# Long and short weight products in turns of one instead of two, in the second layer's gate and value stage

## The chip, the cores and the metric

The kernel runs on one NeuronCore of a Trainium2 chip. The metric is the device time of one execution in microseconds; lower is better.

## The reference

A trunk of two layers works on 256 tokens of width 2048, in float32. Each layer has a token mixer (a causal convolution module in the first, differential attention in the second) and then a gated feed-forward part of width 5504:

```python
def conv_ffn(x, w_gate, w_up, dw, dw_b, w_down):
    g = causal_dwconv(x @ w_gate, dw, dw_b)        # width 3, over tokens
    return (jax.nn.silu(g) * (x @ w_up)) @ w_down
```

The change touches the two products `x @ w_gate` and `x @ w_up` of the second layer.

## The kernel before

**Precision.** Every float32 operand of a product is split in two: a rounded part (type fp32r, made by ScalarE) and the remainder (made by VectorE). A product is then the sum of high x high, high x low and low x high. `w_hi` and `w_lo` hold the two parts of the weights, in four buffers of 1024 columns (`PIECES`); `normed` holds the two parts of the activations side by side, 256 columns of high part and 256 of low part for each of 16 tiles of 128 channels.

**The stages.** The work goes through nine stages: conv_in, conv_out, up0, down0, qk, v, wo, up1, down1. A block is 16 weight tiles of 128 x 128 (1 MB); SyncE's DMA queue brings blocks in order into four buffers (`stage`). For each half block ScalarE writes the high part (`hi`, line 553, after a wait that the buffer's last user is done: `pieces_done`), then VectorE the remainder (`lo`, line 903), then TensorE uses both.

**Two kinds of product on TensorE.** In conv_in, conv_out, down0, v, wo and down1 the activations are the stationary operand and 512 columns of weights are moved through the array: three products of 512 columns for each tile (lines 1532 to 1534, in v 1798 to 1800). In up0, qk and up1 the weights are stationary, in `block_mm`: for each of 16 tiles a long product moves all 512 columns (high and low part of the activations) through `w_hi` (`high_product`, line 1498), and a short one moves the 256 columns of the high part through `w_lo` (`low_product`, line 1503), into the second half of the same PSUM bank. Every product loads its own stationary tile first (records PEld). At the block's end ScalarE copies the second half out (line 565), VectorE adds it to the first (lines 1225 and 1254) and does the gate's convolution and the gating (lines 1235 to 1263), and ScalarE its activation (line 772).

**The order of the products.** `block_mm` waits for the PSUM bank (`evacuated`), and for each half block of 8 tiles for VectorE's remainder (`lo_ready`, line 1481). Then it runs tiles in groups of two: long, long, short, short. The last short product of a half block increments `pieces_done`, which gives the weight buffer back to ScalarE.

**The loops.** The stage up1 has 86 blocks, gate and value in turns: four in a first turn written out (the function `up`), 20 turns of four in a loop on the engines (`pe.Fori(1, KF // 2)`, KF = 43), and two at the end. up0 is the same code with the first layer's weights, qk has 32 blocks.

Of the kernel before, what the change touches and what calls it, by code (L numbers as in the profile page):

```python
# [122 lines left out]
def trunk(nc, x_in, positions, norm_mix, norm_ffn, norm_final, conv_w_in, conv_b_in, conv_dw, conv_dw_b,  # L123
# [7 lines left out]
    KD, KF, TB = D // P, F // P, T // P  # L131
# [15 lines left out]
    B, C = {}, {}  # L147
# [41 lines left out]
    with ExitStack() as ctx:  # L189
        def sb(name, shape, dt=F32, stack=ctx):  # L190
            return stack.enter_context(nc.sbuf_tensor("sb_" + name, shape, dt))
# [14 lines left out]
        normed = sb("normed", [P, KD, 2 * T], F32R)  # L206
# [1264 lines left out]

        @block.tensor
        def _(pe):
            def block_mm(i, blocks_per_turn, block_n, chunk_n, operand, arrivals=(), halfway=None):


                bank = chunk_n % BANKS
                pe.wait_ge(evacuated, 4 * i + chunk_n + 1)
                k = 0
                for h in range(2):  # L1480
                    pe.wait_ge(lo_ready, 2 * blocks_per_turn * i + 2 * block_n + h + 1)
                    slot = (2 * block_n + h) % PIECES
                    if h == 1 and halfway:
                        halfway()
                    for q in range(0, KD // 2, 2):
                        for p in (q, q + 1):
                            for tile, count in arrivals:
                                if tile == k + p:
                                    pe.wait_ge(operand_ready, count)
                            high_product(bank, slot, p, operand, k + p, k + p == 0)  # L1490
                        for p in (q, q + 1):
                            ins = low_product(bank, slot, p, operand, k + p, k + p == KD - 1)
                    k += KD // 2
                    ins.then_inc(pieces_done, 1)

            def high_product(bank, slot, q, operand, k, begin):

                nc.tensor.matmul(acc[:, bank, :], w_hi[:, slot, q * P:(q + 1) * P], operand[:, k, :],  # L1498
                                 start=begin, stop=False, skip_group_check=True)

            def low_product(bank, slot, q, operand, k, end):

                return nc.tensor.matmul(acc[:, bank, T:2 * T], w_lo[:, slot, q * P:(q + 1) * P],  # L1503
                                        operand[:, k, 0:T], start=False, stop=end, skip_group_check=True)
# [57 lines left out]
            def turn_resid(name, c):  # L1562

                n = STAT[name]
                pe.wait_ge(evacuated, BANKS + C[name] + TB * (c + 1))
                if c > 0:

                    pe.wait_ge(operand_ready, OPER[name] + 4 * c)
                for f in range(4):
                    k = 4 * c + f  # L1570
                    for b in range(TB):
                        ins = nc.tensor.transpose(aux[:, f, b * P:(b + 1) * P], resid[:, b, k * P:(k + 1) * P],  # L1572
                                                  ident[:, :])
                    ins.then_inc(resid_turned, 1)
# [10 lines left out]
            def stat(n):  # L1585

                pe.wait_ge(diag_row_ready, TB * n)
                for b in range(TB):
                    ins = nc.tensor.matmul(aux[:, 3, T + b * P:T + (b + 1) * P], ones[:, :], diag_row[:, b, :],
                                           start=True, stop=True)  # L1590
                ins.then_inc(stat_ready, 1)
# [24 lines left out]
            def turn_taps(n):  # L1616

                if n == 0:
                    pe.wait_ge(taps_ready, 2)
                    pe.wait_ge(operand_ready, OPER["x"] + KD)  # L1620
                if n >= BANKS:
                    pe.wait_ge(taps_kept, n + 1 - BANKS)
                nc.tensor.matmul(aux[0:HALF, n % BANKS, :], kern_op[:, n % 2, 0:HALF],
                                 taps_op[:, WIDE * (n // 2):WIDE * (n // 2 + 1)], start=True, stop=True
                                 ).then_inc(taps_turned, 1)
# [19 lines left out]
            def forward(c, rows=range(TB)):  # L1645

                if c == 0:
                    pe.wait_ge(dft_ready, 1)
                    pe.wait_ge(par_kept, 3)
                elif c < CH - 1:  # L1650
                    pe.wait_ge(conv_kept, TB * c)
                for b in rows:
                    pe.wait_ge(glu_split, TB * c + b + 1)
                    for m in range(2):
                        triple(aux[0:HALF, 2 * b + m, :], (dft_hi[:, m, 0:HALF], dft_lo[:, m, 0:HALF]),
                               (glu_op[:, b, 0, :], glu_op[:, b, 1, :]), True, True).then_inc(forward_done, 1)

            def inverse(c, banks):

                for b in range(TB):  # L1660
                    for source in range(b + 1):
                        for m in range(2):
                            at = 2 + 2 * (b - source) + m
                            pe.wait_ge(prod_split, 4 * c + 2 * source + m + 1)
                            ins = triple(banks[:, b, :], (dft_hi[0:ROWS, at, :], dft_lo[0:ROWS, at, :]),
                                         (prod_op[0:ROWS, source, m, 0, :], prod_op[0:ROWS, source, m, 1, :]),
                                         source == 0 and m == 0, source == b and m == 1)
                        if b and source == 0:
                            ins.then_inc(source_done, 1)
                    ins.then_inc(inverse_done, 1)  # L1670
# [13 lines left out]
            for at in range(len(ORDER["conv_in"])):  # L1684
                c, j = divmod(at, 8)
                halfway = None
                if at in TAP_TURNS:
                    halfway = lambda: [turn_taps(n) for n in TAP_TURNS[at]]
                elif at == 9:
                    halfway = turn_params  # L1690
                elif c > 0 and j == 2:
                    halfway = lambda: forward(c - 1)
                elif 0 < c < CH - 1 and j == 5:
                    halfway = lambda: inverse(c - 1, aux)
# [35 lines left out]
            def up(name, before):  # L1730

                arrivals = [(0, OPER[name] - 4)] + [(KD - 4 + f, OPER[name] - 3 + f) for f in range(4)]
                block_mm(0, 4, B[name], C[name], normed, arrivals, lambda: turn_resid(before, CH - 1))
                block_mm(0, 4, B[name] + 1, C[name] + 1, normed, halfway=lambda: stat(STAT[before]))
                for j in range(2, 4):
                    block_mm(0, 4, B[name] + j, C[name] + j, normed)
                with pe.Fori(1, KF // 2) as i:
                    for j in range(4):
                        block_mm(i, 4, B[name] + j, C[name] + j, normed)
                for j in range(2):  # L1740
                    block_mm(KF // 2, 4, B[name] + j, C[name] + j, normed)

            def down(name, hidden_name, turn=True):
                base = OPER[hidden_name]
                project(name, hidden, KF, [(0, base + KF - 3), (KF - 3, base + KF - 2), (KF - 2, base + KF - 1),
                                           (KF - 1, base + KF)], turn=turn)

            up("up0", "conv_out")
            down("down0", "up0")

# [92 lines left out]
            def last_heads(at, k):  # L1843
# [5 lines left out]
                elif (at, k) == (1, 1):  # L1849
# [3 lines left out]
                                           (KD - 4, OPER["wo"] - 2),  # L1853
                                           (KD - 2, OPER["wo"])], last_heads)
            up("up1", "wo")
            down("down1", "up1", False)

# [29 lines left out]
```

## Time and profile before

| | |
|---|---|
| median of 3 runs | 2146.43 us (2146.39 to 2147.22) |
| the profiled execution, its own time | 2146.78 us |
| its span | 2145.0 us |
| granted TensorE clock, mean over the span | 1.000 |
| instructions | 30522 |

The profile is one execution. Its span goes from the first to the last instruction; its own time has 1.78 us more around it. PE is TensorE's matmuls, PEld its weight loads, which overlap with matmuls; DVE is VectorE, ACT is ScalarE. Matmuls overlap in the records too: a product's record is longer than the distance to the next one's start, so their spacing is read from starts, not from lengths.

### The profile page before, as it was taken

The numbers are of one execution on the slowest core, as the hardware profiler recorded it, in microseconds if no ns is written. First come the engines' busy times: TensorE is split into PE (matmuls) and PEld (weight loads), VectorE is DVE, ScalarE is ACT, GpSimd is POOL, SyncE is SP. The second block draws the span as 40 slices with busy tenths as digits, with TensorE's granted clock in tenths as the row PEclk, the third lists the DMA queues.
The fourth block names the chain that finished last, engine by engine and source line by source line (L and its number), as shares of the span: only waits on it lengthen the run. The fifth ranks groups of instructions, "written<-read, shape, count | busy, mean of one in ns | idle before, by whom it ended". The sixth has DMA issues, their size and how long they took to land.

```text
span 2145.0 us, 30522 instructions
## 1 busy us (share of the span) xinstructions
PE 2128.6 (99%) x11045; PEld 1815.1 (85%) x11045; DVE 1449.8 (68%) x2130; ACT 1052.2 (49%) x1492; POOL 48.9 (2%) x50
## 2 busy tenths in 40 slices
PE   8999999999999999999999999999999999999998
PEld 7888888888888888888888888888888888888886
DVE  6666767777777774454688867667777777765443
ACT  6554655445444443444554444554444544444443
POOL 7100000000000000000000000000000000000000
PEclk9999999999999999999999999999999999999999
DMA  8555366666666665555656554566666666656553
GB/s 302 176 185 196 128 186 177 195 182 191 188 185 194 185 188 191 192 190 191 189 165 176 180 176 155 193 180 186 186 194 183 190 189 184 194 195 212 191 191 113
DMA packets 513804, 399.07 MB, mean 186 GB/s; under 512 B 6542, under 2 KB 425832, under 8 KB 513392
## 3 DMA queue, kind: packets, MB, share of 16 engines
q1 hardware_dynamic: 513408, 397.91, 60.1%
q8 instruction: 42, 0.69, 0.1%
q10 hardware_dynamic: 336, 0.33, 0.0%
q14 instruction: 18, 0.15, 0.0%
HBM read 396.11 MB, written 2.10 MB: 186 GB/s over the span
## 4 chain that ended last, share of the span: by engine, by line
PE 97%; DVE 2%; ACT 1%; DMA 0%; issue 0%; SPq 0%; DVEq 0%; ACTq 0%
PE acc L1498 35%; PE acc L1503 18%; PE acc L1532 12%; PE acc L1534 12%; PE acc L1533 12%; PE acc L1800 1%; PE acc L1798 1%; PE acc L1799 1%; DVE sb_w_lo L903 1%; PE aux L1572 0%; DMA sb_stage<-in_conv_w_in 0%; PE aux L1641 0%; PE aux L1642 0%; PE aux L1643 0%; PE aux L1809 0%; PE aux L1757 0%
## 5 line engine op out<-in xcount | busy, mean ns | idle before, releaser
L903 DVE TENSOR_TENSOR sb_w_lo<-sb_stage,sb_w_hi 128x1024 fp32r<-128x1024 f32 (+1 forms) x743 | 906.4, 1222 | 519.1 <-ACT sb_w_hi L553 514.6
L553 ACT ACTIVATE sb_w_hi<-sb_stage 128x1024 fp32r<-128x1024 f32 (+1 forms) x743 | 780.5, 1053 | 661.4 <-PE acc L1534 380.5
L1498 PE MATMUL acc<-sb_normed,sb_w_hi 128*128 128x512 f32 x3264 | 1027.4, 396 | 0.0
L1503 PEld LDWEIGHTS acc<-sb_normed,sb_w_lo 128*128 128x128 f32 x3264 | 613.1, 188 | 144.9
L1503 PE MATMUL acc<-sb_normed,sb_w_lo 128*128 128x256 f32 x3264 | 641.4, 278 | 0.0
L1498 PEld LDWEIGHTS acc<-sb_normed,sb_w_hi 128*128 128x128 f32 x3264 | 497.7, 189 | 0.6
L1532 PE MATMUL acc<-sb_w_hi,sb_hidden 128*128 128x512 f32 x674 | 262.5, 389 | 0.0
L1534 PE MATMUL acc<-sb_w_hi,sb_hidden 128*128 128x512 f32 x674 | 262.2, 389 | 0.0
L1533 PE MATMUL acc<-sb_w_lo,sb_hidden 128*128 128x512 f32 x674 | 262.2, 389 | 0.0
L565 ACT ACTIVATE sb_corr<-acc 128x256 f32<-128x256 f32 x204 | 76.9, 377 | 210.7 <-PE acc L1503 210.6
L1534 PEld LDWEIGHTS acc<-sb_w_hi,sb_hidden 128*128 128x128 f32 x674 | 126.5, 188 | 26.4
L1533 PEld LDWEIGHTS acc<-sb_w_lo,sb_hidden 128*128 128x128 f32 x674 | 126.5, 188 | 26.3
L1532 PEld LDWEIGHTS acc<-sb_w_hi,sb_hidden 128*128 128x128 f32 x674 | 126.5, 188 | 25.9
L772 ACT ACTIVATE sb_acted<-sb_scaled,sb_par_f 128x256 f32<-128x256 f32 x86 | 44.0, 512 | 135.2 <-DVE sb_scaled L1245 135.2
L1245 DVE SCALAR_TENSOR_TENSOR sb_scaled<-sb_gate_in,sb_par_f,sb_scaled 128x256 f32<-128x256 f32 x172 | 83.4, 485 | 24.0 <-DVE sb_scaled L1242 3.2
L1532 PE MATMUL acc<-sb_w_hi,sb_normed 128*128 128x512 f32 x248 | 97.1, 391 | 2.4 <-DVE sb_normed L917 2.4
L1533 PE MATMUL acc<-sb_w_lo,sb_normed 128*128 128x512 f32 x248 | 96.6, 390 | 0.0
L1534 PE MATMUL acc<-sb_w_hi,sb_normed 128*128 128x512 f32 x248 | 96.6, 389 | 0.0
L1225 DVE TENSOR_TENSOR sb_summed<-acc,sb_corr 128x256 f32<-128x256 f32 x86 | 36.5, 425 | 73.8 <-ACT sb_corr L565 73.8
L1532 PEld LDWEIGHTS acc<-sb_w_hi,sb_normed 128*128 128x128 f32 x248 | 46.6, 188 | 12.5 <-DVE sb_w_lo L903 2.8
L1534 PEld LDWEIGHTS acc<-sb_w_hi,sb_normed 128*128 128x128 f32 x248 | 46.6, 188 | 9.8
L1533 PEld LDWEIGHTS acc<-sb_w_lo,sb_normed 128*128 128x128 f32 x248 | 46.6, 188 | 9.6
(215 smaller groups left out, 1647.5 us busy)
## 6 DMA issues: line engine op xcount, KB each, us to landing
sb_stage<-in_ffn_w_gate SPq DMA_DIRECT2D x86, 1024.0 KB, 5.4
sb_stage<-in_ffn_w_up SPq DMA_DIRECT2D x86, 1024.0 KB, 5.5
sb_stage<-in_ffn_w_down SPq DMA_DIRECT2D x80, 1024.0 KB, 5.0
sb_stage<-in_attn_w_qkv SPq DMA_DIRECT2D x48, 1024.0 KB, 5.4
sb_stage<-in_conv_w_in SPq DMA_DIRECT2D x31, 1024.0 KB, 5.6
sb_stage<-in_conv_w_out SPq DMA_DIRECT2D x16, 1024.0 KB, 5.1
sb_stage<-in_attn_w_o SPq DMA_DIRECT2D x16, 1024.0 KB, 5.0
sb_stage<-in_ffn_w_down SPq DMA_DIRECT2D x8, 768.0 KB, 4.4
```

Of the source, the lines that this page charges most:

```text
L553: nc.scalar.activation(w_hi[:, (2 * first + h) % PIECES, 0:size], stage[:, first % STAGES, off:off + size], ACT.Copy).then_inc(hi_ready, 1)
L565: nc.scalar.activation(corr[:, chunk_n % BANKS, :], acc[:, chunk_n % BANKS, T:2 * T], ACT.Copy).then_inc(corr_ready, 1)
L772: nc.scalar.activation(acted[:, e, :], scaled[:, e, :], ACT.Silu, bias=par_f[:, layer, bass.ds(FTAPS * KF + f, 1)]).then_inc(gate_acted, 1)
L903: nc.vector.tensor_tensor(w_lo[:, slot, 0:size], stage[:, first % STAGES, off:off + size], w_hi[:, slot, 0:size].bitcast(F32), ALU.subtrac ...
L1225: nc.vector.tensor_tensor(summed[:, 0, :], acc[:, (C[name] + 2 * e) % BANKS, 0:T], corr[:, (C[name] + 2 * e) % BANKS, :], ALU.add).then_in ...
L1245: ins = nc.vector.scalar_tensor_tensor(out=scaled[:, e, :], in0=x, scalar=w, in1=scaled[:, e, :], op0=ALU.mult, op1=ALU.add)
L1498: nc.tensor.matmul(acc[:, bank, :], w_hi[:, slot, q * P:(q + 1) * P], operand[:, k, :], start=begin, stop=False, skip_group_check=True)
L1503: return nc.tensor.matmul(acc[:, bank, T:2 * T], w_lo[:, slot, q * P:(q + 1) * P], operand[:, k, 0:T], start=False, stop=end, skip_group_c ...
L1532: nc.tensor.matmul(acc[:, bank, :], high, w_hi[:, slot, wide], start=k == 0, stop=False)
L1533: nc.tensor.matmul(acc[:, bank, :], high, w_lo[:, slot, wide], start=False, stop=False)
L1534: ins = nc.tensor.matmul(acc[:, bank, :], low, w_hi[:, slot, wide], start=False, stop=k == tiles - 1)
L1798: nc.tensor.matmul(acc[:, bank, :], high, w_hi[:, slot, wide], start=k == 0, stop=False)
```

## The change

A new argument of `block_mm`, `single`, sets the group to one tile, so that long and short products alternate: long, short, long, short. It is passed in the loop of `up` for the second layer's stage (`name == "up1"`) alone; the first turn and the last two blocks of that stage, and the stages up0 and qk, keep groups of two. No instruction is added or left out, and waits and increments stay where they are.

```diff
-            def block_mm(i, blocks_per_turn, block_n, chunk_n, operand, arrivals=(), halfway=None):
+            def block_mm(i, blocks_per_turn, block_n, chunk_n, operand, arrivals=(), halfway=None, single=False):
...
-                    for q in range(0, KD // 2, 2):
-                        for p in (q, q + 1):
+                    group = 1 if single else 2
+                    for q in range(0, KD // 2, group):
+                        for p in range(q, q + group):
                             for tile, count in arrivals:
                                 if tile == k + p:
                                     pe.wait_ge(operand_ready, count)
                             high_product(bank, slot, p, operand, k + p, k + p == 0)
-                        for p in (q, q + 1):
+                        for p in range(q, q + group):
                             ins = low_product(bank, slot, p, operand, k + p, k + p == KD - 1)
...
                 with pe.Fori(1, KF // 2) as i:
                     for j in range(4):
-                        block_mm(i, 4, B[name] + j, C[name] + j, normed)
+                        block_mm(i, 4, B[name] + j, C[name] + j, normed, single=name == "up1")
```

## Rows read from the trace of the kernel before

**Rows 1.** The page's busy time by engine: us (share of span) xinstructions

```profile
PE 2128.6 (99%) x11045; PEld 1815.1 (85%) x11045; DVE 1449.8 (68%) x2130; ACT 1052.2 (49%) x1492; POOL 48.9 (2%) x50
```

**Rows 2.** The page's chain that ended last, shares of the span by line

```profile
PE acc L1498 35%; PE acc L1503 18%; PE acc L1532 12%; PE acc L1534 12%; PE acc L1533 12%; PE acc L1800 1%; PE acc L1798 1%; PE acc L1799 1%; DVE sb_w_lo L903 1%; PE aux L1572 0%; DMA sb_stage<-in_conv_w_in 0%; PE aux L1641 0%; PE aux L1642 0%; PE aux L1643 0%; PE aux L1809 0%; PE aux L1757 0%
```

**Rows 3.** Busy time by stretch, the loop of up1 (columns in the first line)

```profile
core 0: us, PE busy (x) PEld busy (x) DVE busy (x) ACT busy (x) POOL busy (x), PEclk, DMA share, GB/s
...
1444.80:1890.70 445.90, 445.90 (x2563) 389.05 (x2562) 332.87 (x521) 219.85 (x321) 0.00 (x0) 1.00 0.65 189
```

**Rows 4.** Groups of instructions, same stretch: busy us, mean ns | idle before us

```profile
L1498 PE MATMUL acc<-sb_normed,sb_w_hi 128*128 128x512 f32 x1281 | 402.4, 395 | 0.0
L1503 PE MATMUL acc<-sb_normed,sb_w_lo 128*128 128x256 f32 x1282 | 251.8, 278 | 0.0
L1503 PEld LDWEIGHTS acc<-sb_normed,sb_w_lo 128*128 128x128 f32 x1280 | 240.4, 188 | 56.8
L903 DVE TENSOR_TENSOR sb_w_lo<-sb_stage,sb_w_hi 128x1024 fp32r<-128x1024 f32 x161 | 197.0, 1224 | 58.1 <-ACT sb_w_hi L553 57.9
L1498 PEld LDWEIGHTS acc<-sb_normed,sb_w_hi 128*128 128x128 f32 x1282 | 195.1, 189 | 0.0
L553 ACT ACTIVATE sb_w_hi<-sb_stage 128x1024 fp32r<-128x1024 f32 x160 | 169.2, 1057 | 91.8 <-PE acc L1503 91.8
```

**Rows 5.** Waits in the same stretch: us in total, times, longest

```profile
ACT sb_w_hi L553 <- PE acc L1503: 91.8, 80, 1.4
...
DVE sb_w_lo L903 <- ACT sb_w_hi L553: 57.9, 119, 0.8
```

**Rows 6.** Timeline of TensorE (start us, us, what), the loop's first and next products

```profile
1444.82 0.63 PE L1498 MATMUL acc<-sb_normed,sb_w_hi 128*128 128x512 f32 x2
...
1890.68 0.63 PE L1498 MATMUL acc<-sb_normed,sb_w_hi 128*128 128x512 f32 x2
```

**Rows 7.** Timeline, nine products of the loop in order, one by one

```profile
1499.85 0.40 PE L1498 MATMUL acc<-sb_normed,sb_w_hi 128*128 128x512 f32 x1
1500.09 0.39 PE L1498 MATMUL acc<-sb_normed,sb_w_hi 128*128 128x512 f32 x1
1500.32 0.28 PE L1503 MATMUL acc<-sb_normed,sb_w_lo 128*128 128x256 f32 x1
1500.43 0.28 PE L1503 MATMUL acc<-sb_normed,sb_w_lo 128*128 128x256 f32 x1
1500.55 0.40 PE L1498 MATMUL acc<-sb_normed,sb_w_hi 128*128 128x512 f32 x1
1500.78 0.40 PE L1498 MATMUL acc<-sb_normed,sb_w_hi 128*128 128x512 f32 x1
1501.02 0.28 PE L1503 MATMUL acc<-sb_normed,sb_w_lo 128*128 128x256 f32 x1
1501.13 0.27 PE L1503 MATMUL acc<-sb_normed,sb_w_lo 128*128 128x256 f32 x1
1501.24 0.40 PE L1498 MATMUL acc<-sb_normed,sb_w_hi 128*128 128x512 f32 x1
```

**Rows 8.** Timeline, the down projection of the second layer, 180 products apart

```profile
2000.00 0.39 PE L1533 MATMUL acc<-sb_w_lo,sb_hidden 128*128 128x512 f32 x1
...
2040.80 0.39 PE L1533 MATMUL acc<-sb_w_lo,sb_hidden 128*128 128x512 f32 x1
```

**Rows 9.** Timeline, the down projection's first product and its seventh

```profile
1901.83 0.40 PE L1532 MATMUL acc<-sb_w_hi,sb_hidden 128*128 128x512 f32 x1
...
1903.21 0.39 PE L1532 MATMUL acc<-sb_w_hi,sb_hidden 128*128 128x512 f32 x1
```

**Rows 10.** Timeline, first groups of qk, behind the first layer's down projection

```profile
1036.84 0.62 PE L1498 MATMUL acc<-sb_normed,sb_w_hi 128*128 128x512 f32 x2
...
1037.52 0.63 PE L1498 MATMUL acc<-sb_normed,sb_w_hi 128*128 128x512 f32 x2
...
1038.22 0.62 PE L1498 MATMUL acc<-sb_normed,sb_w_hi 128*128 128x512 f32 x2
```

**Rows 11.** Timeline, two weight loads beside the products of rows 7

```profile
1500.32 0.19 PEld L1503 LDWEIGHTS acc<-sb_normed,sb_w_lo 128*128 128x128 f32 x1
1500.43 0.19 PEld L1498 LDWEIGHTS acc<-sb_normed,sb_w_hi 128*128 128x128 f32 x1
```

## The prediction

> **What bounds the kernel now.** I begin with the page's busy line: TensorE's matmuls are busy for 2128.6 of 2145.0 us [rows 1], and the chain that ended last runs through TensorE for nearly its whole length, 35% of the span at the long products of the routine that the change edits and 18% at its short ones [rows 2]. A busy share of 99% alone would not prove a bound, since matmul ends are modelled, so the second thing to look at is whether TensorE ever waits in the stage of the change. The stretch from 1444.80 to 1890.70 us holds the loop of the second layer's gate and value stage: matmuls cover all 445.90 us of it, at a granted clock of 1.00 (the 2.4 GHz level), while VectorE works 332.87 us and ScalarE 219.85 us [rows 3]. The groups of that stretch say the same: no idle time is recorded ahead of either product, each product has a weight load of its own whose record is 188 or 189 ns long, and the makers of the weights (ScalarE's rounded copy, VectorE's remainder) do 169.2 and 197.0 us of work [rows 4]. The list of waits has ScalarE waiting 91.8 us for TensorE to give back weight buffers, and VectorE 57.9 us for ScalarE; nothing is on it that TensorE waits for [rows 5]. So the stage lasts exactly as long as TensorE needs to run its queue of loads and products, and the only thing in this edit that can move the time is the spacing of those products.
>
> **How they are spaced.** The first long product of the loop starts at 1444.82 us and the first one behind the loop at 1890.68 us [rows 6]: 445.86 us. The loop is 20 turns of 4 blocks of 16 tiles, 1280 tiles, so 1280 long (512 columns) and 1280 short products (256 columns); in groups of two long and two short that is 640 groups of 445.86 / 640 = 0.6967 us. Inside two groups, product by product [rows 7]: long to long takes 0.24 and 0.23 us, long to short 0.23 and 0.24, short to short 0.11 and 0.11, short to long 0.12 and 0.11, together 1.39 us. Starts are printed to 10 ns, so each difference is good to 10 ns only, and I use sums.
>
> **The change, part by part.** It removes no instruction and adds none. In each of the 640 groups, long long short short becomes long short long short. One long-to-long and one short-to-short step go, and one more long-to-short and one more short-to-long step come. By the steps' means, what goes costs 0.235 + 0.11 = 0.345 us and what comes 0.235 + 0.115 = 0.35 us. That is +5 ns per group, 640 x 0.005 = +3.2 us, and it is smaller than the rounding of the rows it is made of. The other estimate is that nothing changes: each group still holds two long and two short products and four loads, each load still runs beside the product ahead of it, and two of the four are still beside a short one. I take the middle of 0 and 3.2, **+1.6 us**.
>
> Three things move with the order and cost nothing. The wait for VectorE's remainder stands ahead of each half block, before the first product, so a short product that comes one place sooner meets no wait of its own; what covers it is that TensorE finds both weight buffers ready every time [rows 4, 5]. The increment that frees a buffer stays on the half block's last short product, so ScalarE's next copy, VectorE's remainder and the DMA queue behind them see the same moments. The instruction count of the loop body is the same. If the stage became shorter by the largest amount below, 10.7 us, VectorE would have 332.87 us of work in some 435 us [rows 3], so no other engine takes over the bound.
>
> **The bounds of the unknown.** The trace of before has no alternating stretch in this routine, so the spacing is bounded from both sides. The nearest undisturbed rows are the down projection's, where all products have 512 columns: 180 of them in 2040.80 - 2000.00 = 40.80 us, 0.2267 us each [rows 8]. At that rate for each column a short product is 0.1133 and a group 2 x 0.2267 + 2 x 0.1133 = 0.680 us. The real group is 0.6967, so some 16.7 ns of each group is lost to something that the mixture brings, 640 x 0.0167 = 10.7 us in the stage. Two readings are possible, and they have opposite signs. If the loss belongs to changes of length (two in a group now, four afterwards), it doubles: +10.7 us. If it belongs to two short products in a row, it goes: -10.7 us. If it belongs to each short product, whatever stands beside it, it stays: 0.
>
> Two places speak about this. Behind the loop's stage, where the down projection begins, six products of 512 columns take 1903.21 - 1901.83 = 1.38 us, 0.230 each [rows 9], more than the settled 0.2267: what short products leave behind is paid over several long ones, and so is not tied to the step from one length to the other. Where the first layer's projection meets a stage of this kind, the first group after long products only takes 1037.52 - 1036.84 = 0.68 us and the next 0.70 [rows 10]: the first change from long to short is free, and the loss builds up from short products onwards. Both favour "belongs to each short product" over "belongs to each change of length". They don't exclude either, and the second leaves room for "two short ones in a row".
>
> **Rivals.**
> (A) The forecast: the spacing is a property of the mixture. +1.6 us, bounds 0 and +3.2.
> (B) The slower side: every step from one length to the other costs its share of the loss, 8.3 ns, and the change adds two to each group, 1280 in all: +10.7 us, 2157.1 us. Its place is the loop's short-to-long and long-to-short steps. It decides (over 0.2%, 4.3 us) from 3.4 ns for each added step. For it: the short-to-long step is printed as 0.12 in one group of two and as 0.11 in the other, against 0.11 twice for short to short [rows 7], and a group takes 0.6967 where the rate for each column gives 0.680. Against it: the free first change [rows 10].
> (C) The faster side: the second of two short products starts late since its load has only a short product to hide behind, and the one after it too; with a long product ahead of each short one there is slack. At best the whole loss goes: -10.7 us, 2135.7 us. Against it: the load for a product is seen to start together with the product ahead of it, never sooner: that for the second short one at 1500.32 with the first short product, that for the next long one at 1500.43 with the second [rows 7, 11]. So an alternating order gives loads no longer runway in sum; short-to-short is also the step without any visible stretch (0.11 against 0.1133).
> On this case the Trainium skill (TensorE: Matmul & The Clock Gate, Part 2, on LDWEIGHTS) says that a queue of 64 lets the engine pull weight loads ahead of products in flight, into a background buffer. If loads could run several places ahead, rival C would come out at its full 2135.7 us. By that rule the trace does not agree here: loads begin with the product ahead, not sooner.
> (D) The edit reaches nothing: the test on the stage's name or the loop's place could leave the order as it was. As written it applies to 80 of that stage's 86 blocks, so this has a chance of 2 in 100 and the time of before; it is inside "same".
>
> **How the numbers follow.** The sum is made against the profiled execution, which took 2146.78 us by its own time, 1.78 us around its span of 2145.0. The median of the three runs is 2146.43, 0.35 us below it, so the same +1.6 us on the median gives 2146.43 + 1.6 = 2148.0 us. About 0.2%, 4.3 us, is what a measurement of this kernel can tell from no change. Chances: 0.58 for A (D within it): a deviation of under 3.4 ns for an added step. 0.29 for B or a part of it that exceeds 4.3 us, since an untried order can only disturb a stream that already loses time after short products, and nothing in the rows excludes it. 0.13 for C or a part of it that exceeds 4.3 us; the start of the loads speaks against it. The range reaches up to B's full price, 2157.1, rounded to 2157.5, and down to 2143.0, a quarter to a third of C; that leaves out most of C (about 0.12) and a B above its price (about 0.05).
>
> **What would show it.** In the changed kernel's timeline the loop should show every product alone, long and short in turns. Right for A: two neighbours, long and short, start 0.348 to 0.351 us apart from the next pair, so the loop's first and the first long product behind it are 445.9 to 449.1 us apart; TensorE still has no recorded idle time, the waits of ScalarE for TensorE in the loop stay near 92 us, and the first layer's stage and the down projection keep their length. For B, pairs are 0.357 us apart and the long product behind a short one is the one that stretches; for C, 0.340. The prediction would be wrong in kind if TensorE showed a wait at the start of a half block, if the granted clock fell below 1.00 in the loop, or if a stage other than this one moved.

## The result, and the profile after

The changed kernel takes 2153.81 us (median of 8 runs, 2152.28 to 2154.32), the kernel before 2147.04 us (8 runs, 2145.89 to 2147.53, the three from above among them): 6.8 us more, ratio 1.0031 with a 95% interval of 1.0023 to 1.0040. It is slower by more than the 0.2% that a measurement of this kernel can tell from no change. It lies in the stated range (2143.0 to 2157.5), but on the side that had a chance of 0.29.

The profiled execution took 2153.85 us, with a span of 2152.0 us against 2145.0. The page's busy line still has TensorE at 99%:

```profile
PE 2136.4 (99%) x11045; PEld 1818.8 (85%) x11045; DVE 1448.9 (67%) x2130; ACT 1051.8 (49%) x1492; POOL 48.0 (2%) x50
```

Against [rows 1] only TensorE's busy times have grown, by 7.8 us for matmuls and 3.7 for weight loads, and a busy share doesn't tell a product that runs longer from one that starts later. The place is found with the timeline of TensorE. The loop's first product and the first one behind it (one product, the long one is now line 1499, the short one 1504):

```profile
1445.48 0.40 PE L1499 MATMUL acc<-sb_normed,sb_w_hi 128*128 128x512 f32 x1
...
1897.75 0.40 PE L1499 MATMUL acc<-sb_normed,sb_w_hi 128*128 128x512 f32 x1
```

The loop takes 1897.75 - 1445.48 = 452.27 us, where [rows 6] give 445.86: 6.41 us more, of the 7.0 by which the span grew. Behind it nothing has moved (254.25 us to the end of the span, 254.32 before). The rest, 0.66 us, lies ahead of the loop, in code that didn't change; over all the kernels below, whose code is the same up to there save one, the loop's first product starts between 1443.69 and 1445.58 us, so that is what executions differ by. Part of it may be the clock: in this trace the granted clock is 0.50 from 18.8 to 22.1 us, and in the trace of before it is 1.00 all the way from 6.2 us to the loop.

The busy time of the loop's stretch (stretch, length, then busy us and number of each engine as in [rows 3]), its main groups, and its waits:

```profile
1445.50:1897.80 452.30, 452.30 (x2563) 392.15 (x2562) 332.82 (x521) 219.56 (x322) 0.00 (x0) 1.00 0.64 186
```

```profile
L1499 PE MATMUL acc<-sb_normed,sb_w_hi 128*128 128x512 f32 x1281 | 452.7, 399 | 0.0
L1504 PE MATMUL acc<-sb_normed,sb_w_lo 128*128 128x256 f32 x1282 | 359.9, 281 | 0.0
L1504 PEld LDWEIGHTS acc<-sb_normed,sb_w_lo 128*128 128x128 f32 x1280 | 241.8, 189 | 0.0
L1499 PEld LDWEIGHTS acc<-sb_normed,sb_w_hi 128*128 128x128 f32 x1282 | 240.8, 188 | 60.2
```

```profile
ACT sb_w_hi L553 <- PE acc L1504: 98.4, 80, 1.4
...
DVE sb_w_lo L903 <- ACT sb_w_hi L553: 62.8, 120, 0.8
```

The same products and loads as in [rows 4], the granted clock still 1.00, VectorE's 332.82 us and ScalarE's 219.56 us of work unchanged, and no idle time recorded ahead of a product. ScalarE's wait for TensorE grew from 91.8 [rows 5] to 98.4 us, by 6.6: the others wait out what TensorE takes longer. A trap is in the groups: the short products' busy time went from 251.8 to 359.9 us [rows 4] with a mean that moved from 278 to 281 ns. Busy time is counted once where records overlap, and two short products in a row overlap each other; alternating ones don't. It is no extra work. What counts is the distance between starts:

```profile
1500.26 0.40 PE L1499 MATMUL acc<-sb_normed,sb_w_hi 128*128 128x512 f32 x1
1500.49 0.28 PE L1504 MATMUL acc<-sb_normed,sb_w_lo 128*128 128x256 f32 x1
1500.60 0.40 PE L1499 MATMUL acc<-sb_normed,sb_w_hi 128*128 128x512 f32 x1
1500.84 0.28 PE L1504 MATMUL acc<-sb_normed,sb_w_lo 128*128 128x256 f32 x1
1500.95 0.40 PE L1499 MATMUL acc<-sb_normed,sb_w_hi 128*128 128x512 f32 x1
1501.19 0.28 PE L1504 MATMUL acc<-sb_normed,sb_w_lo 128*128 128x256 f32 x1
1501.32 0.40 PE L1499 MATMUL acc<-sb_normed,sb_w_hi 128*128 128x512 f32 x1
```

Three pairs take 1501.32 - 1500.26 = 1.06 us, 0.3533 each (452.27 / 1280 gives the same), where half a group of two and two took 0.3483. Long to short is 0.23, 0.24 and 0.24, short to long 0.11, 0.11 and 0.13. The increase is 5.0 ns a pair and so 5.0 ns for each of the 1280 added steps, above the 3.4 ns at which rival B was to decide and below its 8.3.

### The profile page after: what moved, and what is told of

Read it like the earlier page. It is cut to its first block, busy times and chain, and to the rows that moved or that the text cites. A ratio compares the mean times of both kernels' runs of the same rounds, so it can differ in the third digit from the quotient of the medians.

```text
span 2152.0 us, 30522 instructions
## 1 busy us (share of the span) xinstructions
PE 2136.4 (99%) x11045; PEld 1818.8 (85%) x11045; DVE 1448.9 (67%) x2130; ACT 1051.8 (49%) x1492; POOL 48.0 (2%) x50
## 4 chain that ended last, share of the span: by engine, by line
PE 98%; DVE 0%; DMA 0%; ACT 0%; SPq 0%; issue 0%; DVEq 0%
PE acc L1499 35%; PE acc L1504 18%; PE acc L1533 12%; PE acc L1535 12%; PE acc L1534 12%; PE acc L1801 1%; PE acc L1800 1%; PE acc L1799 1%; PE aux L1573 0%; DMA sb_stage<-in_conv_w_in 0%; PE aux L1642 0%; PE aux L1643 0%; PE aux L1644 0%; PE aux L1810 0%; PE aux L1758 0%; DVE sb_w_lo L903 0%
## 5 line engine op out<-in xcount | busy, mean ns | idle before, releaser
L1499 PE MATMUL acc<-sb_normed,sb_w_hi 128*128 128x512 f32 x3264 | 1077.7, 397 | 0.0
L1504 PE MATMUL acc<-sb_normed,sb_w_lo 128*128 128x256 f32 x3264 | 749.5, 279 | 0.0
L1499 PEld LDWEIGHTS acc<-sb_normed,sb_w_hi 128*128 128x128 f32 x3264 | 543.4, 188 | 60.7
```

## The experiments

All start from the changed kernel and alter the loop of the second layer's stage alone, unless said otherwise. Loop times are read as above, from the first product of the loop to the first one behind it, by TensorE's timeline. `g4` and `g8` were executed ten times and `both` four times; each other kernel was executed once. A loop time is always that of one execution, and loops with the same order repeat closely: 445.86 and 445.87 us in the second and first layer of the kernel before, 452.27, 452.27 and 452.28 in the changed kernel, in `sbank` and in the first layer of `both`, all with turns of one.

**Other turns.** Is it a price for each change of length? `g4` and `g8` run longer rows of one length.

```diff
-                    group = 1 if single else 2
+                    group = 4 if single else 2        # g4; g8: 8
```

> The loop of the second layer's stage runs four long, then four short products. Theory S (each step from one length to the other costs a fixed time): turns of one cost 6.4 us more than turns of two in the profile, for 1280 added steps, 5.0 ns each. Turns of four have 640 steps fewer than turns of two: the loop gets 3.2 us shorter than the 445.9 us of before, 442.7 us. Theory N (something peculiar to a product whose both neighbours have the other length, such as the load of a long product behind a lone short one, and no price for steps as such): turns of four are like turns of two, 445.9 us.

> The loop runs the eight long products of a half block, then its eight short ones. Theory S: 960 steps fewer than in turns of two, 4.8 us less, 441.1 us for the loop. Theory N: 445.9 us. Theory L (two short products in a row cost something that grows with the row, since the loads have only short products to hide behind): turns of four and of eight are slower than turns of two, by more for eight.

g4's loop, then g8's:

```profile
1444.43 0.40 PE L1499 MATMUL acc<-sb_normed,sb_w_hi 128*128 128x512 f32 x1
...
1893.50 0.40 PE L1499 MATMUL acc<-sb_normed,sb_w_hi 128*128 128x512 f32 x1
```

```profile
1445.40 0.40 PE L1499 MATMUL acc<-sb_normed,sb_w_hi 128*128 128x512 f32 x1
...
1892.34 0.40 PE L1499 MATMUL acc<-sb_normed,sb_w_hi 128*128 128x512 f32 x1
```

449.07 and 446.94 us. Theory S wanted 442.7 and 441.1, theory N 445.9 for both, theory L more for eight than for four. None of them holds as a whole (theory L is right only in that both are slower than turns of two): with a quarter of the changes of turns of two, turns of eight still take 1.1 us more than those, and turns of four 3.2 us more. Whole kernels: g4 2149.52 us, ratio to before 1.0014 (1.0004 to 1.0023); g8 2147.89 us, 1.0004 (0.9994 to 1.0013), not told from before.

**What a product costs when all have one length.** In `all512` the short product is made as long as the long one, in `all256` the long one as short.

```diff
-                            ins = low_product(...)
+                            ins = nc.tensor.matmul(acc[:, bank, :], w_lo[:, slot, p * P:(p + 1) * P],
+                                                   operand[:, k + p, 0:2 * T], ...)          # all512
...
-                            high_product(...)
+                            nc.tensor.matmul(acc[:, bank, 0:T], w_hi[:, slot, p * P:(p + 1) * P],
+                                             operand[:, k + p, 0:T], ...)                    # all256
```

> Turns of one as in the changed kernel, but in the loop the product with the weights' remainder moves all 512 columns too (it adds remainder x remainder to the result). All products have one length while weights' parts, banks and order stay as in turns of one. Theory S: no loss is left, 0.2267 us for each product as in the down projection, so the loop takes 2560 x 0.2267 = 580.3 us. Theory W (the alternation of the two weight tensors as stationary operand, or that one activation tile is moved twice in a row, costs time): the 5 ns for each added step stay, 0.2317 us or more, 593 us.

> Turns of one, but in the loop the long products move only the 256 columns of the high part (high x low is left out). All products have one length, 256. Theory S with a cost in proportion to columns: 0.1133 us each, 290.1 us for the loop. Theory F (a fixed loss for each short product, which its weight load sets): more than 0.1133 each; to explain the 16.7 ns lost in a group of two long and two short it would have to be 0.1217 us, 311 us for the loop. As far as TensorE waits for VectorE's and ScalarE's copies here, the spacing is read from half blocks without a wait.

all512, the loop:

```profile
1444.95 0.40 PE L1504 MATMUL acc<-sb_normed,sb_w_hi 128*128 128x512 f32 x1
...
2025.25 0.39 PE L1504 MATMUL acc<-sb_normed,sb_w_hi 128*128 128x512 f32 x1
```

all256, one product and the one 16 places behind it (line 1509 is the product with the remainder):

```profile
1456.98 0.28 PE L1509 MATMUL acc<-sb_normed,sb_w_lo 128*128 128x256 f32 x1
...
1458.90 0.28 PE L1509 MATMUL acc<-sb_normed,sb_w_lo 128*128 128x256 f32 x1
```

all512 takes 580.30 / 2560 = 0.2267 us a product, exactly the down projection's pace [rows 8]. This stream has the order of the changed kernel and one length. So alternating the two weight tensors and moving one activation tile twice in a row costs nothing: theory W falls, the loss needs two lengths. all256 takes 1.92 / 16 = 0.120 us a product (its loop as a whole is 361.6 us, as TensorE waits for VectorE's remainders there). Neither of the two figures expected for it came (0.1133 and 0.1217); theory F was right only in that it is more than 0.1133. This is the key number of the study. From 512 to 256 columns a product gets 0.1067 us shorter, which is 256 columns at 2.4 GHz; both are 13.3 ns longer than their columns. For these two lengths the cost is **columns / 2.4 GHz + 13.3 ns**, not in proportion to columns. A group of two and two without loss, which here means at the pace of streams of one length, is then 2 x 0.2267 + 2 x 0.120 = 0.6933 us and not 0.680, and the loop 443.7 us. Turns of two lose 3.3 ns a group of four, not 16.7.

**PSUM.** In `sbank` the short product writes a bank that nothing else uses.

```diff
-                            ins = low_product(...)
+                            ins = nc.tensor.matmul(aux[:, 1, T:2 * T], w_lo[:, slot, p * P:(p + 1) * P],
+                                                   operand[:, k + p, 0:T], start=k + p == 0, ...)
```

> Turns of one in the loop, the short products writing a PSUM bank of their own that nobody reads (so low x high is left out of the result). Theory B (the loss comes from a short product adding to columns that the long one before it has just written, and the long one after it adding there again): the pair goes from 0.3533 to the lossless 0.3467, the loop from 452.3 to 443.7 us. Theories P and C: no change, 452.3 us.

```profile
1444.08 0.40 PE L1504 MATMUL acc<-sb_normed,sb_w_hi 128*128 128x512 f32 x1
...
1896.35 0.40 PE L1504 MATMUL acc<-sb_normed,sb_w_hi 128*128 128x512 f32 x1
```

452.27 us, to the digit that of the changed kernel. Theory B falls: adding to columns just written has no part in it.

**Turns of three.** `g332`:

```diff
+                    for turn in ((0, 1, 2), (3, 4, 5), (6, 7)) if single else ((0, 1), (2, 3), (4, 5), (6, 7)):
+                        for p in turn:
```

> The eight tiles of a half block run in turns of three, three and two. Lossless would be 2.773 us for a half block; turns of two lose 13 ns of it, of one 53, of four 33, of eight 20. If the loss is paid over the long products behind each row of short ones, 3 long products pay about 7 + 9 + 1 ns less the 6.7 that the first short one gains, some 10 to 14 ns a turn: 30 to 35 ns for a half block, loop 449 us. If turns of two are a point of their own between two trends and the loss for each change falls with the length of the turn: at most 13 ns, 445.9 us or less.

```profile
1445.39 0.40 PE L1498 MATMUL acc<-sb_normed,sb_w_hi 128*128 128x512 f32 x1
...
1892.86 0.40 PE L1498 MATMUL acc<-sb_normed,sb_w_hi 128*128 128x512 f32 x1
```

447.47 us, between its two expectations (449 and at most 445.9), so it settles neither working; it does say that turns of two are better than turns of three as well.

**Other lengths.** `s384`, `s128` and `s496` run turns of one, `p384` turns of two, with short products of 384, 128 and 496 columns.

```diff
-                            ins = low_product(...)
+                            ins = nc.tensor.matmul(acc[:, bank, P:2 * T], w_lo[:, slot, p * P:(p + 1) * P],
+                                                   operand[:, k + p, 0:3 * P], ...)          # s384, p384
+                            # s128: acc[:, bank, T:T + P], 0:P;  s496: acc[:, bank, 16:2 * T], 0:2 * T - 16
```

> Turns of one in the loop, but the short product moves 384 columns instead of 256 (into the wrong columns, so that its sum is not the reference's). Without loss, by the equal-length runs (0.2267 us for 512 columns, 0.120 for 256, so 0.1733 for 384), a pair takes 0.400 us and the loop 512.0 us. Theory P (the loss arises since a 256-column product is no longer than the weight load it has to hide): with 384 columns there is slack, no loss, 512.0 us. Theory C (any change of length costs): the loss of turns of one stays, 5.1 ns a pair and more, 518.5 us.

> Turns of two in the loop, short products of 384 columns (added to the wrong columns). Lossless a group of two and two takes 0.800 us, the loop 512.0. Theory E (each product that starts before the stream has settled after a change of length costs up to 6.7 ns more, whatever the turns): in turns of one that was 6.7 ns for each product, and here, where half the products follow one of another length, it is the same or slightly less: 0.820 to 0.827 us, 525 to 529 us. Theory G (a price for each change, 6.7 ns with 384 columns): two changes a group, 0.8133 us, 520.5 us. If turns of two have a peculiar advantage that doesn't depend on lengths: 0.803, 514 us.

> Turns of one, short products of 496 columns (added to the wrong columns), almost as long as the long ones. Lossless a pair takes 0.2267 + 0.2200 = 0.4467 us and the loop 571.7. If any inequality keeps the stream from settling, the loss is the 13.3 ns a pair of the 384-column run: 0.460 us, 588.8 us. If the loss depends on how far the two lengths are apart: between these, near 571.7 us.

> Turns of one, short products of 128 columns (half the low part's share left out). The run with 128 columns throughout had products 0.1117 us apart at the granted clock 1.00, which is then the pace of the weight loads and not of the columns (0.067). So lossless a pair takes 0.2267 + 0.1117 = 0.3383 us, the loop 433.1 us; with the loss of turns of one at 256 columns (6.7 ns a pair) 0.345, 441.6 us. If a long product's slack hid part of the load of the product behind the short one, a pair would get down to 0.2267 + 0.080 = 0.3067 us, 392.5 us.

s384, the loop, and then p384:

```profile
1445.09 0.40 PE L1504 MATMUL acc<-sb_normed,sb_w_hi 128*128 128x512 f32 x1
...
1974.14 0.40 PE L1504 MATMUL acc<-sb_normed,sb_w_hi 128*128 128x512 f32 x1
```

```profile
1443.69 0.40 PE L1504 MATMUL acc<-sb_normed,sb_w_hi 128*128 128x512 f32 x1
...
1972.75 0.40 PE L1504 MATMUL acc<-sb_normed,sb_w_hi 128*128 128x512 f32 x1
```

s496, the loop, and then s128:

```profile
1444.52 0.40 PE L1504 MATMUL acc<-sb_normed,sb_w_hi 128*128 128x512 f32 x1
...
2016.30 0.39 PE L1504 MATMUL acc<-sb_normed,sb_w_hi 128*128 128x512 f32 x1
```

```profile
1444.96 0.40 PE L1504 MATMUL acc<-sb_normed,sb_w_hi 128*128 128x512 f32 x1
...
1880.12 0.44 PE L1504 MATMUL acc<-sb_normed,sb_w_hi 128*128 128x512 f32 x1
```

529.05, 529.06, 571.78 and 435.16 us. No stream of 384 or of 496 columns alone was run; their base is taken from the line through 512 and 256 columns, 0.1733 and 0.2200 us. By it, with 384 columns, where the weight load has more slack, the loss is larger, 13.3 ns a pair: theory P (a short product that is no longer than its load) falls as the cause. Whatever the base, the time is the same in turns of two as in turns of one, the upper end of theory E, so the advantage of turns of two is not general, it belongs to 512 with 256. With 496 columns nothing is lost, so not every inequality costs. With 128 the loss is 2.1 us over the loop, against a base that is an assumption (next experiment).

The losses over the loop, each against 2560 products of columns / 2.4 GHz + 13.3 ns (for 128 columns against 0.1117 us, the pace of the next experiment), worked out before rounding:

| short product | turns | loop, us | without loss, us | loss, us |
|---|---|---|---|---|
| 512 | one | 580.3 | 580.3 | 0.0 |
| 496 | one | 571.8 | 571.7 | 0.0 |
| 384 | one | 529.1 | 512.0 | 17.1 |
| 384 | two | 529.1 | 512.0 | 17.1 |
| 256 | one (the change) | 452.3 | 443.7 | 8.5 |
| 256 | two (before) | 445.9 | 443.7 | 2.1 |
| 256 | three, three, two | 447.5 | 443.7 | 3.7 |
| 256 | four | 449.1 | 443.7 | 5.3 |
| 256 | eight | 446.9 | 443.7 | 3.2 |
| 128 | one | 435.2 | 433.1 | 2.1 |

17.1 us on 2560 products is 6.7 ns each, 16 columns at 2.4 GHz, half of the 13.3 ns that products of 256 and 512 columns have beyond their columns.

The loss is a balance of two amounts. In a mixed stream the step from a long product to the next one is longer than in a stream of one length, and the step from a short product is shorter. Means over the 1280 steps of each kind, from the starts of the loop's products in each trace:

| 512 and 256 columns | step from a long product, ns | step from a short product, ns |
|---|---|---|
| one length each | 226.7 | 120.0 |
| turns of one | 236.3 | 117.1 |
| turns of two | 233.1 | 115.2 |
| turns of eight | 230.1 | 119.1 |

In turns of two a long product's step is 6.5 ns longer and a short one's 4.8 ns shorter, so most of what the long ones lose comes back.

**The pace of weight loads.** `all128` runs all products of the loop with 128 columns.

```diff
+                                nc.tensor.matmul(acc[:, bank, 0:P], w_hi[:, slot, p * P:(p + 1) * P],
+                                                 operand[:, k + p, 0:P], ...)
...
+                                ins = nc.tensor.matmul(acc[:, bank, T:T + P], w_lo[:, slot, p * P:(p + 1) * P],
+                                                       operand[:, k + p, 0:P], ...)
```

> Turns of one, all products of the loop with 128 columns (large parts of the sums left out). Read within half blocks, where nothing is waited for. Theory P: the weight load sets the pace, products start 0.120 us apart or little less. If instead a product costs 13.3 ns and its columns whatever its load takes: 0.067 us. TensorE will wait for the copies at half blocks, and its clock may fall; spacing is read at the granted clock 1.00.

Its timeline at granted clock 1.00, two products 16 places apart (line 1499 is the product with the remainder):

```profile
1456.97 0.27 PE L1499 MATMUL acc<-sb_normed,sb_w_lo 128*128 128x128 f32 x1
...
1458.76 0.27 PE L1499 MATMUL acc<-sb_normed,sb_w_lo 128*128 128x128 f32 x1
```

1.79 / 16 = 0.112 us, where 128 columns and 13.3 ns would be 0.067, so something other than the columns sets the pace. The load of the next weights is the likely one; no run separates it from another cost that each product has. A 256-column product at 0.120 is 8 ns above it, so, read in this way, no product of 256 or 512 columns here is held up by its load, though the margin is small. In `s128` this pace doesn't hold for each step:

```profile
1500.00 0.44 PE L1504 MATMUL acc<-sb_normed,sb_w_hi 128*128 128x512 f32 x1
1500.28 0.22 PE L1494 MATMUL acc<-sb_normed,sb_w_lo 128*128 128x128 f32 x1
1500.34 0.44 PE L1504 MATMUL acc<-sb_normed,sb_w_hi 128*128 128x512 f32 x1
```

The short product starts 0.28 us behind the long one and the next long one 0.06 us behind the short one. Their sum, 0.340, is close to 0.2267 + 0.1117, but that sum as the time without loss is an assumption. The clock fell in `all128`, as told below.

**The same change in the first layer.** `both` passes `single=True` in that stage too.

```diff
-                        block_mm(i, 4, B[name] + j, C[name] + j, normed, single=name == "up1")
+                        block_mm(i, 4, B[name] + j, C[name] + j, normed, single=True)
```

> Turns of one in the loops of both layers' gate and value stages. If the loss is a matter of the order of products and of nothing else in its surroundings, the first layer's loop, the same code with other weights, takes the same 6.4 us more that the second one's did, and the whole kernel 13 us more than before: about 2160 us, ratio 1.006. If the second layer's stage was special (its place, its buffers, what runs beside it), the first layer's loop gets another amount, and the ratio stays near 1.003.

The first layer's loop in the kernel before, then in this one:

```profile
343.15 0.40 PE L1498 MATMUL acc<-sb_normed,sb_w_hi 128*128 128x512 f32 x1
...
789.02 0.40 PE L1498 MATMUL acc<-sb_normed,sb_w_hi 128*128 128x512 f32 x1
```

```profile
343.42 0.40 PE L1499 MATMUL acc<-sb_normed,sb_w_hi 128*128 128x512 f32 x1
...
795.70 0.40 PE L1499 MATMUL acc<-sb_normed,sb_w_hi 128*128 128x512 f32 x1
```

445.87 and 452.28 us: 6.41 us more, the amount of the second layer's loop. The whole kernel takes 2158.9 us against 2146.33, ratio 1.0057 (1.0040 to 1.0073), which fits the expected 1.006. The loss is a matter of the order of products and of nothing around it.

## Why the prediction was right and wrong

**Right: where to look.** TensorE bounds the stage, no wait was added, the other engines wait 6.6 us longer in ScalarE's line instead of setting the pace, the clock stayed, other stages kept their length (the first layer's loop takes 789.68 - 343.82 = 445.86 us). All of the time is in the spacing of products, as said; the run in the first layer confirms it a second time.

**Wrong: the likeliest case.** A, with its +1.6 us, fell; 6.4 us came. The step that failed is the sum over steps, "what goes costs 0.345 us and what comes 0.35 us". It took the cost of long-to-short and short-to-long from a stream of two and two and put it into a stream of one and one. The steps don't keep their price. Averaged over all starts of the loop, long to short was 233.3 ns before and is 236.3 after, short to long was 115.8 and is 117.1. That is 4.2 ns a pair, 5.3 us in the loop. The sum itself was sized well: with the same means of before (long to long 232.9, short to short 114.6) it gives +1.7 ns a group, 1.1 us. The two together are the 6.4 us. So the failure is not the rounding of the two groups of [rows 7]; it is that steps of one order were taken to price another, which a trace of before alone can't settle.

**Wrong: the base of the bounds.** "At that rate for each column a short product is 0.1133": it is 0.120, since the 13.3 ns beyond the columns don't shrink with them. So the loss of a group was put at 16.7 ns where it is 3.3, and both rivals' prices came from that. Rival C could have gained at most 2.1 us, if a mixed stream is never faster than streams of one length; it could not have reached the 4.3 us to which its chance of 0.13 was tied. [rows 10] were read by the same base: the first group of qk, 0.686 us by its unrounded starts, looked nearly free of loss against 0.680, and it is 7 ns shorter than 0.6933, since the step from its first short product is 113 ns instead of 120. The upper bound of 10.7 us was right in size only by chance. With 3.3 ns lost at two changes a group, a price for each change would have doubled to +2.1 us, and the true 6.4 would have lain outside.

**Rival B had the sign, not the mechanism.** "Every step from one length to the other costs its share" is refuted by turns of four and of eight, which have fewer steps than turns of two and lose more, and by 384 columns, where halving the steps saves nothing. The sentence on [rows 9], that what short products leave behind is paid over several long ones, was nearer: in turns of eight the eight long ones of this stretch of g8 take 1503.11 - 1501.27 = 1.84 us, against 8 x 0.2267 = 1.81:

```profile
1501.27 2.00 PE L1499 MATMUL acc<-sb_normed,sb_w_hi 128*128 128x512 f32 x8
1503.11 1.11 PE L1504 MATMUL acc<-sb_normed,sb_w_lo 128*128 128x256 f32 x8
```

That explains why turns of eight are no gain. That two and two lose so little is then a matter of the short steps, which get shorter nearly as much as the long ones get longer; why they do is not shown.

**The load's runway.** The argument against C, that a load is seen to start with the product ahead of it, stands in the changed kernel (loads at 1500.49 and 1500.61, products at 1500.49 and 1500.60), and in the loops of all the kernels above no load starts before the product ahead of it. The rule of the Trainium skill (TensorE: Matmul & The Clock Gate, Part 2, on LDWEIGHTS) that loads are pulled ahead of products in flight is seen here only as far as one place:

```profile
1500.49 0.19 PEld L1499 LDWEIGHTS acc<-sb_normed,sb_w_hi 128*128 128x128 f32 x1
1500.61 0.19 PEld L1504 LDWEIGHTS acc<-sb_normed,sb_w_lo 128*128 128x128 f32 x1
```

**What stays open.** Why a mixed stream loses, and why so unevenly: none of weight tensor, activation tile, PSUM bank, load length or number of changes explains the table. The loop times show one regularity. Divided by their number of repeating groups they are whole multiples of 3.33 ns (8 columns at 2.4 GHz) within 0.1 ns: a pair in turns of one takes 353.33 ns, 106 of them, where 104 would be without loss; a group of two and two 209 for 208, of four and four 421 for 416, of eight and eight 838 for 832, a half block in turns of three, three and two 839 for 832, pairs with 384 and 496 columns 124 and 134. That suggests that starts fall on some grid and that a repeating order either fits it or not. No experiment tested this, and it doesn't say how many steps of the grid an order loses.

No order that was run beats the kernel before. Turns of two are the best of the five in loop time, and the most that any order could still save is 2.1 us a loop, as long as no mixed stream beats the pace of streams of one length.

## What to carry to other kernels

From 256 to 512 columns the cost of a product here was a fixed part and a part for its columns; get the two from two streams of one length each before using either as a base, because a rate for each column from the longest product underrates the short ones. In this stream, bound by TensorE, the order of products of different lengths was worth up to 1.4% of the loop and 0.3% of the kernel without any wait in the trace. It was neither additive in the steps nor monotonic in the length of the turns, and no order's price followed from another's: each had to be run. A loop's length, from the first product to the first behind it, resolved 1 us in 2147 here where whole-kernel runs needed several repeats.

## What the runs showed of the hardware

In `all128` the granted clock fell to half in the loop (stretch, length, busy us of PE, PEld, DVE, ACT, POOL with their numbers, then the granted clock):

```profile
1455.40:1462.50 7.10, 7.10 (x66) 7.10 (x65) 6.21 (x11) 3.96 (x6) 0.00 (x0) 1.00 0.71 204
1462.50:1465.40 2.90, 1.50 (x14) 1.36 (x13) 2.40 (x4) 2.19 (x4) 0.00 (x0) 1.00 1.03 299
1468.00:1480.00 12.00, 12.00 (x58) 12.00 (x58) 10.24 (x18) 5.74 (x9) 0.00 (x0) 0.50 0.86 254
1600.00:1750.00 150.00, 150.00 (x705) 150.00 (x705) 92.54 (x143) 61.23 (x89) 0.00 (x0) 0.50 0.53 154
1978.00:1980.00 2.00, 2.00 (x13) 1.79 (x12) 0.47 (x2) 0.48 (x1) 0.00 (x0) 0.94 0.60 89
```

Before it fell, TensorE had run 128-column products 0.112 us apart, with one wait for weights: in the second stretch it is idle for 1.4 us, which ended at 1464.3 us, and the clock fell at 1466.2. Whether that wait or the short products made it fall is not shown. In `all256` TensorE waited for VectorE's remainders 37 times, up to 1.1 us each, and the granted clock stayed at 1.00. In `all128` it stayed at 1.2 GHz for the rest of the loop, although matmuls were busy for all 150.00 us of the fourth stretch, and came back once products of 512 and 256 columns had followed. At the low clock the products are 0.213 us apart (705 in 150 us), so the loop took longer than with twice the columns: products of half the length made the kernel slower, 2232.55 us against 2063.34 of `all256` (530.0 us against 361.6 for the loop). A busy share of 100% is thus no sign that the clock is at its upper level; the granted clock has to be read beside it.
